# Block 2's attention: transposes ahead of the preceding step's value products, and the next maximum ahead of the transposed copies

## The reference

```python
h = rms_norm_2(x, g_mix[l])
proj = h @ w_in[l]
y_a = mla_mixer(...)            # 8 heads, full softmax over 256 keys
y_b = dilated_mixer(...)        # 12 heads in 3 groups: band, every 4th, every 16th key
y_c = neighbourhood_mixer(...)  # 8 heads, 8 x 16 window, with a bias table rpb
gates = sigmoid(gate_logits)
merged = g0 * (y_a @ w_pa[l]) + g1 * (y_b @ w_pb[l]) + g2 * (y_c @ w_pc[l])
x = x + merged @ w_o[l]
x = x + (silu(h2 @ w1[l]) * (h2 @ w3[l])) @ w2[l]     # h2: x, normed again
```

## Time and profile before

| | |
|---|---|
| median of three runs | 1583.63 us (1580.25 to 1584.52) |
| the profiled execution's own time | 1579.04 us |
| its span | 1577.3 us |
| TensorE (PE) busy | 1555.5 us, 99% |
| VectorE (DVE) busy | 1068.8 us, 68% |
| ScalarE (ACT) busy | 769.0 us, 49% |
| GpSimd (POOL) busy | 40.1 us, 3% |
| DMA | 267.24 MB, 169 GB/s over the span |

### The profile page before, as it was taken

How to read it: one execution, slowest core, us unless ns; L and a number is a source line. 1 busy time by engine, 2 the same in 40 slices (tenths; PEclk the granted TensorE clock), 3 DMA queues, 4 the chain that set the end, 5 groups by cost and what they waited for, 6 DMA issues and landing times.

```text
span 1577.3 us, 18675 instructions
## 1 busy us (share of the span) xinstructions
PE 1555.5 (99%) x7644; PEld 1272.9 (81%) x7644; DVE 1068.8 (68%) x1413; ACT 769.0 (49%) x893; POOL 40.1 (3%) x28
## 2 busy tenths in 40 slices
PE   7999999999999999999999999999999999999997
PEld 6888888888888888887777788888887777888886
DVE  4768655566785666966666875656866667876555
ACT  4655444456554444764445354444664444454443
POOL 0000000001000000000020100000000020100000
PEclk9999999999999999999999999999999999999999
DMA  8435555544255554444543455554434643555551
GB/s 296 171 107 186 213 187 187 187 176 171 101 193 190 188 186 173 160 141 138 149 155 134 162 210 189 187 187 150 169 133 159 149 146 123 202 204 192 183 192 54
DMA packets 54246, 267.24 MB, mean 169 GB/s; under 512 B 18705, under 2 KB 19345, under 8 KB 24209
## 3 DMA queue, kind: packets, MB, share of 16 engines
q1 hardware_dynamic: 40784, 262.02, 46.5%
q10 hardware_dynamic: 13376, 4.02, 1.7%
HBM read 264.98 MB, written 1.05 MB: 169 GB/s over the span
## 4 chain that ended last, share of the span: by engine, by line
PE 89%; DVE 7%; ACT 2%; DMA 1%; issue 1%; SPq 0%; DVEq 0%; ACTq 0%
PE psum L412 26%; PE psum L414 26%; PE psum L413 26%; PE psum L450 4%; DVE wl L1272 2%; PE psum L504 1%; PE psum L778 1%; DMA raw<-in_weights 1%; PE psum L817 1%; PE psum L760 1%; PE psum L808 1%; DVE work L1756 1%; ACT wh L900 0%; PE psum L622 0%; PE psum L606 0%
## 5 line engine op out<-in xcount | busy, mean ns | idle before, releaser
L1272 DVE TENSOR_TENSOR wl<-raw,wh 128x2048 fp32r<-128x2048 f32 (+1 forms) x250 | 561.8, 2250 | 277.1 <-ACT wh L900 274.1
L900 ACT ACTIVATE wh<-raw 128x2048 fp32r<-128x2048 f32 (+1 forms) x250 | 467.2, 1873 | 403.2 <-PE psum L414 394.2
L412 PE MATMUL psum<-wh,xh 128*128 128x512 f32 (+1 forms) x1632 | 647.8, 397 | 9.0 <-ACT work L934 3.0
L414 PE MATMUL psum<-wh,xl 128*128 128x512 f32 (+1 forms) x1632 | 633.3, 388 | 0.0
L413 PE MATMUL psum<-wl,xh 128*128 128x512 f32 (+1 forms) x1632 | 632.5, 388 | 0.0
L412 PEld LDWEIGHTS psum<-wh,xh 128*128 128x128 f32 x1632 | 307.3, 188 | 81.7 <-issue 16.8
L414 PEld LDWEIGHTS psum<-wh,xl 128*128 128x128 f32 x1632 | 307.2, 188 | 63.2
L413 PEld LDWEIGHTS psum<-wl,xh 128*128 128x128 f32 x1632 | 307.8, 189 | 57.4
L412 PE MATMUL psum<-wh,ah 128*128 128x512 f32 (+1 forms) x360 | 140.4, 390 | 0.0
L414 PE MATMUL psum<-wh,al 128*128 128x512 f32 (+1 forms) x360 | 139.3, 387 | 0.0
L413 PE MATMUL psum<-wl,ah 128*128 128x512 f32 (+1 forms) x360 | 139.2, 387 | 0.0
(11 more groups left out here) (169 smaller groups left out, 1067.0 us busy)
## 6 DMA issues: line engine op xcount, KB each, us to landing
raw<-in_weights SPq DMA_DIRECT2D x234, 1024.0 KB, 4.9
raw<-in_weights SPq DMA_DIRECT2D x10, 512.0 KB, 3.6
raw<-in_weights SPq DMA_DIRECT2D x4, 832.0 KB, 4.3
arena<-in_rpb ACTq DMA_DIRECT2D x32, 96.0 KB, 8.7
raw<-in_weights SPq DMA_DIRECT2D x8, 256.0 KB, 6.8
raw<-in_weights SPq DMA_DIRECT2D x2, 768.0 KB, 5.2
x<-in_x SPq DMA_DIRECT2D x4, 256.0 KB, 4.5
out<-arena SPq DMA_DIRECT2D x3, 256.0 KB, 3.1
```

What stands on the lines that cost most here:

```text
L412: nc.tensor.matmul(dst, lh, right(wh, slot), start=start, stop=False)
L414: return nc.tensor.matmul(dst, ll, right(wh, slot), start=False, stop=stop)
L900: nc.scalar.activation(wh[:, slot, 0:n], raw[:, slot, 0:n], ACT.Copy).then_inc(high_ready.sem, 1)
L1272: nc.vector.tensor_tensor(wl[:, slot, 0:n], raw[:, slot, 0:n], wh[:, slot, 0:n].bitcast(F32), ALU.subtract).then_inc(split_ready.sem, 1)
```

## The change

In `attend` the transposes of step m are issued ahead of the value products of m-1, but for the last step, which keeps its order. On VectorE the maximum of m+1 moves ahead of the copy of m's transposes (and of the output, and of nothing else). This second part also keeps the copy from writing `prob_t` while the value products of m-1 still read it: the maximum waits for the scores of m+1, which TensorE issues behind those value products. No instruction is added or removed, and no data changes.

```diff
                 def attend(m):
+                    if m == STEPS - 1:
+                        weighted(m - 1)
+                        probs_t(m)
+                        return
+                    probs_t(m)
                     if m >= 1:
                         weighted(m - 1)
-                    probs_t(m)
...
                     if m < STEPS - 1:
+                        row_max(m + 1)
                         probs_out()
                     if m >= 1 and (m - 1) % 4 == 3 and m != 20:
                         output((m - 1) // 4)
                     if m + 1 < STEPS:
-                        row_max(m + 1)
                         if m in (5, 7):
```

## The result

The change makes the kernel slower: 1594.11 us (1591.93 to 1596.78, four runs) against 1581.97 us (1580.25 to 1584.52, four runs), with a recorded ratio of 1.0088 and a 95% interval of 1.0072 to 1.0104. The two medians themselves differ by 12.1 us, a quotient of 1.0077; a ratio of 1.0088 would be 13.9 us. The forecast was +11.5 us and 1595.1. The profiled execution after took 1591.93 us, 12.9 more than that of before; its span is 1590.2 us, and 1590.5 had been worked out for its time from the single terms.

The account below looks back on a forecast made before the run. TensorE was taken as the bound, holding 89% of the chain that ended last. Terms summed to 5.45 us in layer 0 and 6.05 in layer 1, +11.5 together, carried to the earlier median 1583.63: 1595.1 us, range 1587 to 1600.5.

Parts of the forecast that it names:

- A: Steps m = 0 and 1: later unit sums, with value products now behind the transposes, delay scores: +0.9 us per layer.
- C: Step m = 5: second group of c's query transposes waits for the copy that empties its bank: +1.35 us per layer.
- D: Step m = 7: second group of c's key transposes waits for the bank's copy: +1.35 us per layer.
- m = 8 and 9: Steps where VectorE's list is longest: step 8's 0.15 gain lost, 0.06 for a start after a stop: +0.1 us per layer.
- E: Step m = 14: VectorE stands behind GpSimd's column mask, value products no longer cover: +1.5 us layer 0, +2.1 layer 1.
- m = 10 to 13: Steps 10 to 13 of each layer: forecast -0.15 us, from step 10; step 12's gain was counted as used up by E.
- Tile forms: TensorE spacing where matmul tile form changes: -0.15 us for each step with 64-row scores, with 0.20 taken for unseen neighbours.
- T: Steps m = 20 to 23 and the hand-over, where VectorE is the bound: later unit sums and scores, +1.0 us per layer.
- rival 4: TensorE's new stops let the granted clock fall: given no time, only room above; chance 0.10 shared with Rival 3.
- Rival 1: Only TensorE's order counts: not slower, -3.6 to -4.6 us, 1579 to 1580; chance 0.08.
- Rival 2: Bank waits as computed, but late unit sums hidden (A, E, T near nothing): +4.1 us, 1587.7; chance 0.10.
- Rival 3: GpSimd goes ahead of step 13's unit sums: up to +1.7 us per layer, 1596.8 to 1598.5; chance 0.10 shared with rival 4.

Follow-up runs that it names:

- x2: Changed kernel with the old order in steps with late unit sums (TensorE 1, 14, 20, 21, 22; VectorE 0, 1, 13, 14, 20, 21, 22): 1585.45 us, ratio 1.0032.
- x1: Changed kernel with steps 5 and 7 in the old order on both engines: 1588.41 us, ratio 1.0051 to the kernel before.
- x4: Kernel before with only VectorE's part of the change, TensorE in its old order: 1588.30 us, ratio 1.0050.
- x7: Kernel before with TensorE's new order only in steps 7, 8, 10, 12, 16 to 20, and alternating copy buffers: 1577.41 us, ratio 0.9983.
- x6: Changed kernel with one of GpSimd's four mask instructions per layer, three quarters of mixer c's column mask left out: 1589.98 us, ratio 1.0061.
- x3: Changed kernel with the old-order step sets of x1 and x2 joined: 1579.86 us, ratio 1.0005 to the kernel before.
- x5: Kernel before with only TensorE's part of the change, VectorE in its old order, copies in alternating buffers: 1581.30 us, ratio 1.0006.

## Why the prediction was right

The kernel became slower by the stops that the prediction named. That the sum came so near owes something to luck. Over both layers A, C, D, m = 8 and 9, and m = 15 to 19 came within 0.15 us each. E came 0.9 us below its 3.6; the fall of the clock added 1.2, m = 10 to 13 0.7 and the a steps 0.4, and these had been put at nothing or at a gain. The level had luck too: it was carried from 1583.63, and of the 36 later runs of the kernel before, on two chips, none is above 1582.5 (medians 1580.14 and 1579.54).

- **The bound.** TensorE's starts decided, and every term showed up as a stop or a spacing of its own.
- **Tile forms, -0.15.** Right: -0.13 to -0.16 in every one of these steps, and the distance of 0.20 taken for unseen neighbours was measured at 0.20 wherever no stop stands in front. Step 12 has its -0.15 too (layer 1), which the prediction took as used up by E. The claim that a steps stay level was off by 0.04 to 0.10 in m = 3, 4 and 6.
- **A, +0.9.** Right: 0.84; x2 takes it away with the old order.
- **C and D, +1.35 each.** Right: 1.43 and 1.35; x1 takes away both, and of the other terms only E and m = 10 to 13 of layer 0 are not as after (the mask's phase with the clock, and ScalarE's wait); x4 has both without TensorE's change.
- **m = 8 and 9, +0.1.** Right: the stop of step 9 ate step 8's gain. x7, with VectorE's old order, keeps it.
- **E, +1.5 and +2.1.** The mechanism right, the size not: 1.78 and 0.89, 2.7 in all for 3.6. x6 shows the mechanism. The term of layer 1 was mis-sized because it took GpSimd's start from the profile before; GpSimd started 0.6 later against the step, and VectorE's split slipped through without standing. In layer 0 the lead shrank from 2.7 to 2.3 us, and the term is larger than 1.5 by about as much.
- **T, +1.0.** Right in layer 0 (1.01) and in x6's layer 1 (1.02). Layer 1's 2.2 has the fall of the clock in it, the prediction's rival 4, for which it had left only room.
- **Missing:** ScalarE's DMA issue ahead of the tanh. m = 10 to 13 are at +0.69 in layer 0 where -0.30 stands in layer 1, so about 1.0 us. It comes with the duration of the issue: the last four loads take 4.1 us in x2 and x4, 6.9 in x3 and x5, 7.0 in x1 and x6, 7.2 in x7 and 7.4 after, and step 12 is the later the longer they take. They begin 1.30 us behind the projection in every profile, so the order does not shift them, and x7, whose VectorE order is the old one, has a stop of 0.5. That their length owes anything to the change is not shown.
- **Rival 1** (the order on TensorE alone counts) is what is left when all stops are taken away. x7 is near that case: -2.1 us in the steps of its profile. **Rival 2** (late unit sums stay hidden) is ruled out by A, E and T in the profile after, 7.6 us of the 12.9. **Rival 3** (GpSimd gets in ahead of the unit sums of step 13) did not happen: in layer 0 they began at 801.85 and took their usual 0.62, and GpSimd began at 802.93.

## What to carry to other kernels

An instruction that fills a hole ahead of another wait is free only where it stands; look who waits for its end, and above all for the buffer that it empties, before it is moved behind that wait. Independent work placed in front of a wait is its cover: move it behind, and the wait shows in full, and two such moves can cost more together than the sum of each alone (A: 0.84 for 0.06 and 0.46). Where an order pays in some steps and costs in others, give each step its own order.

## What was not expected of the hardware

- The granted clock fell to half for 3.4 us inside the steps in the profile after (layer 1), in x1 (both layers) and in x6 (layer 0), each time right behind a stop of TensorE of 1.6 to 2.4 us, and cost 1.2 to 1.6 us where it fell. Behind the shorter stops of 1.0 to 1.3 it never did, and in x2, x3, x4, x5 and x7 it did not fall within the steps. But behind four other stops of 1.6 to 1.8 it did not fall either. Eight such stops are too few to say more.
- GpSimd's four adds, 7.4 us of work per layer on an engine 3% busy, cost 2.9 us of the 12.9 by where they fell against two VectorE instructions (step 14 after against x6). A difference of 0.15 us in when the split asks, 3.58 us behind GpSimd's start or 3.73, made the difference between not standing and standing 1.58.
